# Moving 32 sample rows out of a pass of their own into the last prompt group, which is halved (groups of 4, 4, 4, 2 and 2 + sample tiles)

## The reference, cut to what matters

```python
xn = rmsnorm(x, g_mix);  z = xn @ w_in
a, u, v, ga, gb = split(z)                    # widths 512, 512, 512, 1024, 1024
pa = pool_mixer(a, hist, ...)                 # causal windows 2, 4, 8, 16; 15 rows of history
pb = u * (w_spatial (lower triangle) @ rmsnorm(v, g_v) + b_spatial)   # inside chunks of 128 rows
merged = sigmoid(ga) * (pa @ w_up_pool) + sigmoid(gb) * (pb @ w_up_gmlp)
h  = x + merged @ w_out
hn = rmsnorm(h, g_ffn)
y  = rmsnorm(h + moe(hn), g_final)            # 16 experts: best group of 4, then 2 experts in it
```

## Time and profile before

| what | value |
|---|---|
| median of 3 executions | 2057.61 us |
| profiled execution, first to last instruction (span) | 2054.1 us |
| PE busy / share | 1895.9 us / 92% |
| PEld busy / share | 1600.8 us / 78% |
| DVE busy / share | 1034.9 us / 50% |
| ACT busy / share | 832.3 us / 41% |
| mean granted TensorE clock | 0.962 |
| DMA, over the span | 153 GB/s |

### The profile page before, as it was taken

How to read it: one execution, slowest core, us unless ns; L and a number is a source line. 1 busy time by engine, 2 the same in 40 slices (tenths; PEclk the granted TensorE clock), 3 DMA queues, 4 the chain that set the end, 5 groups by cost and what they waited for, 6 DMA issues and landing times. The chain is left out here.

```text
span 2054.1 us, 28746 instructions
## 1 busy us (share of the span) xinstructions
PE 1895.9 (92%) x9892; PEld 1600.8 (78%) x9893; DVE 1034.9 (50%) x2051; ACT 832.3 (41%) x1564; POOL 283.8 (14%) x388
## 2 busy tenths in 40 slices
PE   6999999999999999999997764999999999999980
PEld 5788888888878888888885543888888888888870
DVE  4644455544454544555444654454456454546434
ACT  4333333333343333333323553444446454446423
POOL 2000000010000010000100202222222222222223
PEclk9999999999999999999997886999999999999995
DMA  6332333323342223522334575585566576656428
GB/s 213 123 100 85 139 140 132 103 92 135 123 145 96 90 83 131 173 77 95 103 123 166 169 250 168 149 268 162 155 224 218 169 264 191 184 174 215 142 53 340
DMA packets 173306, 316.24 MB, mean 154 GB/s; under 512 B 9757, under 2 KB 92701, under 8 KB 173226
## 3 DMA queue, kind: packets, MB, share of 16 engines
q1 hardware_dynamic: 155754, 255.07, 36.0%
q0 software_dynamic: 15120, 51.59, 10.1%
q10 hardware_dynamic: 2352, 8.52, 1.0%
HBM read 266.09 MB, written 49.07 MB: 153 GB/s over the span
## 5 line engine op out<-in xcount | busy, mean ns | idle before, releaser
L751 DVE TENSOR_TENSOR wl<-raw,wh 128x512 fp32r<-128x512 f32 x440 | 274.3, 685 | 207.2 <-ACT wh L573 205.3
L1597 PE MATMUL bank<-gu_hi,ex_hi 128*128 128x256 f32 (+1 forms) x960 | 310.5, 323 | 4.5 <-DVE gu_lo L1507 4.5
L60 PE MATMUL bank<-xT_hi,wh 128*128 128x512 f32 x768 | 301.0, 392 | 10.6 <-ACT ext L711 7.0
L1599 PE MATMUL bank<-gu_hi,ex_lo 128*128 128x256 f32 (+1 forms) x960 | 307.1, 320 | 0.0
L1598 PE MATMUL bank<-gu_lo,ex_hi 128*128 128x256 f32 (+1 forms) x960 | 306.9, 320 | 0.0
L62 PE MATMUL bank<-xT_hi,wl 128*128 128x512 f32 x768 | 299.4, 390 | 0.0
L61 PE MATMUL bank<-xT_lo,wh 128*128 128x512 f32 x768 | 299.3, 390 | 0.0
L573 ACT ACTIVATE wh<-raw 128x512 fp32r<-128x512 f32 x440 | 240.2, 619 | 99.5 <-PE bank L1140 49.9
L1597 PEld LDWEIGHTS bank<-gu_hi,ex_hi 128*128 128x128 f32 x960 | 183.2, 191 | 23.9 <-DVE gu_lo L1507 6.5
L1599 PEld LDWEIGHTS bank<-gu_hi,ex_lo 128*128 128x128 f32 x960 | 183.2, 191 | 13.3
L1598 PEld LDWEIGHTS bank<-gu_lo,ex_hi 128*128 128x128 f32 x960 | 183.5, 191 | 12.5
(11 more groups left out here) (239 smaller groups left out, 3258.0 us busy)
## 6 DMA issues: line engine op xcount, KB each, us to landing
raw<-in_w_in SPq DMA_DIRECT2D x70, 1024.0 KB
raw_gate_up<-in_w_gate SPq DMA_DIRECT2D x16, 2048.0 KB, 8.4
raw_gate_up<-in_w_up SPq DMA_DIRECT2D x16, 2048.0 KB, 13.4
raw_d<-in_w_down SPq DMA_DIRECT2D x16, 2048.0 KB, 13.0
raw<-in_w_out SPq DMA_DIRECT2D x20, 1024.0 KB
raw<-in_w_up_pool SPq DMA_DIRECT2D x20, 512.0 KB
raw<-in_w_up_gmlp SPq DMA_DIRECT2D x20, 512.0 KB
h<-in_x_prompt SPq DMA_DIRECT2D x16, 512.0 KB, 5.2
```

The source lines that it names most:

```text
L60: nc.tensor.matmul(out, lh, rh, start=(i == 0), stop=False)
L751: lo = lambda out, x, hi: tt(out, x, hi.bitcast(F32), ALU.subtract)
L1597: nc.tensor.matmul(out, a[0][:, ka, :], w[0][:, kw, cols], start=(n == 0), stop=False)
L1599: return nc.tensor.matmul(out, a[1][:, ka, :], w[0][:, kw, cols], start=False, stop=(n == total - 1))
```

## The change

Groups are now `PROMPT_TILES = (4, 4, 4, 2, 2)`, and the last one takes the 32 sample rows as a third, short tile: 256 + 32 = 288 columns. The number of passes (five and the prologue) and of panels stays. Group 3 has 256 columns. `sample_panel`, `to_rows` and their scratch `tm` are gone; `rows` and `rows2` depend on the tile; the prompt's and the sample's pooling rows stand side by side in `ext`, each with its 16 columns of history; the four tables of bank uses come from one function; and the loop over passes 1 and 2 is written out.

```diff
+PROMPT_TILES = (4, 4, 4, 2, 2)
+LAST = len(PROMPT_TILES) - 1
+FIRST_TILE = (0, 4, 8, 12, 14)
+def tiles_in(g):
+    return PROMPT_TILES[g] + (1 if g == LAST else 0)
...
+    @staticmethod
+    def columns(g):
+        return PROMPT_TILES[g] * P + (SAMPLE if g == LAST else 0)
...
-        def passes(eng, body):
-            body(PhaseOne(-1))
-            body(PhaseOne(0))
-            with eng.Fori(1, NPROMPT - 1) as g:
+        def passes(body):
+            for g in range(-1, LAST + 1):
                 body(PhaseOne(g))
-            body(PhaseOne(NPROMPT - 1))
-            body(PhaseOne(NPROMPT))
...
-                if not ph.pro and not ph.next:
-                    pe.wait_ge(sp_read, g * TPG + ph.nt)
-                    for i in range(2):
-                        sample_panel(ph, i, [("u", 2 * i, xT, every)])
-                    for i in range(4):
-                        sample_panel(ph, 2 + 3 * i, [("ga", 2 * i, xT, every)])
-                        sample_panel(ph, 3 + 3 * i, [("gb", 2 * i, xT, every)])
-                        pe.wait_ge(pb_ok, g * 4 + 4)
-                        sample_panel(ph, 4 + 3 * i, [("P", 2 * i, pa, [(k, k) for k in range(4)]),
-                                                     ("Q", 2 * i, pb, [(4 + k, k) for k in range(4)])])
-                elif not ph.pro:
+                if not ph.pro:
                     for i in range(2):
                         for c in range(2):
                             chunk(ph, i, c, "u", 2 * i + c, xT, every, n)
...
                 if not ph.next:
-                    router(ph, 0)
+                    router(ph, ph.nt - 1)
                     count(ph)
                     return
-                if ph.nt2 == 1:
-                    sample_panel(ph, 20, [("a", 0, xT, every)])
-                    router(ph, ph.nt - 1)
-                    sample_panel(ph, 21, [("a", 2, xT, every)])
-                    pool_products(ph, 0)
-                    pool_products(ph, 1)
-                    count(ph)
...
+                pool_products(ph, 1)
+                if ph.places_itself:
+                    count(ph)
...
                     for t in range(min(3, ph.nt)):
-                        if t == min(2, ph.nt) and ph.next:
+                        if t == min(2, ph.nt - 1) and ph.next:
                             split(ph, 19)
                         norm_h(ph, t)
...
                     b = full(act, ph, "a", m)
-                    nc.scalar.activation(exts[m % 2][:, 16:16 + n2], bankA[b][:, 0:n2], ACT.Copy)\
-                        .then_inc(a_free[b], 1)
+                    if ph.last2:
+                        nc.scalar.activation(ext[:, 32 + main:32 + main + SAMPLE], bankA[b][:, main:n2], ACT.Copy)
+                    nc.scalar.activation(ext[:, 16:16 + main], bankA[b][:, 0:main], ACT.Copy).then_inc(a_free[b], 1)
```

More of the change, by code:

```diff
@@ L63, in products, with bank_uses @@
     return last
-def bank_uses(nt, nt_next, first):
+def tiles_in(g):
+    return PROMPT_TILES[g] + (1 if g == LAST else 0)
+def bank_uses(nt, nt_next):
     seq = []
-    if not first:
+    if nt:
         seq += [("u", m) for m in range(4)]
@@ L123, in __init__ @@
-        self.before = None if self.pro else (
-            (LAST_P_USES, N_LAST_P) if static and g == NPROMPT else (MID_USES, N_MID))
+        self.pro = g < 0
+        self.next = g < LAST
+        self.nt = 0 if self.pro else tiles_in(g)
+        self.nt2 = tiles_in(g + 1) if self.next else 0
+        self.n = 0 if self.pro else self.columns(g)
+        self.n2 = self.columns(g + 1) if self.next else 0
+        self.t0 = 0 if self.pro else FIRST_TILE[g]
+        self.first = FIRST_TILE[g + 1] if self.next else NT
@@ L126, in prev, with rows, rows2 @@
+        self.last2 = g + 1 == LAST
+        self.uses, self.start = USES[g][0], USES_BEFORE[g]
+    @staticmethod
+    def columns(g):
+        return PROMPT_TILES[g] * P + (SAMPLE if g == LAST else 0)
+    def rows(self, t):
+        return SAMPLE if self.g == LAST and t == self.nt - 1 else P
+    def rows2(self, t):
+        return SAMPLE if self.last2 and t == self.nt2 - 1 else P
     @property
     def prev(self):
-        return None if isinstance(self.g, int) and (self.g < 1 or self.g == NPROMPT) else PhaseOne(self.g - 1)
+        return None if self.g < 1 or self.g == LAST else PhaseOne(self.g - 1)
@@ L131, in places_itself @@
     @property
     def places_itself(self):
-        return isinstance(self.g, int) and self.g >= NPROMPT - 1
+        return self.g >= LAST - 1
     def use(self, *key):
-        return self._place(self.uses[key])
+        i = self.start + self.uses[key]
+        return i % 2, i // 2
     def use_before(self, *key):
[L142 to L148, removed]
+        i = USES_BEFORE[self.g - 1] + USES[self.g - 1][0][key]
@@ L583, in softmaxes @@
                 act.wait_ge(exps_in, ph.g + 1)
[L584 removed]
+                nc.scalar.activation(exps[:, 0:ph.nt, :], exps[:, 0:ph.nt, :], ACT.Exp)\
                     .then_inc(exps_ok, 1)
[L587 to L595 removed]
             def squares_of_x(ph, tiles):
                 if ph.nt2 and not ph.pro:
[L599 removed]
+                    act.wait_ge(x_in, 16 * (ph.g + 1) + (16 if ph.last2 else 0))
                 for t in tiles:
```

300 lines of the change are left out of this document (123 added, 177 removed).

## The result

The changed kernel takes 2029.87 us (median of 4 runs, 2027.53 to 2030.18), the kernel before, on the same chip, 2058.71 (4 runs, 2056.06 to 2062.48). The ratio is 0.9855, 95% interval 0.984 to 0.9869. The profiled executions have spans of 2028.5 and 2054.1 us, a gain of 25.6 where 39.0 were forecast. The sign was as forecast, and the range of 2003 to 2036 held the time; it lies above the likeliest case's own range (2010 to 2028).

The account below looks back on a forecast made before the run. The sample pass was held by loading and splitting panels, the new passes by PE. Stages from 769.7 fall from 495.1 to 460.3 us, with the loop -39.0: 2015.1 profiled, median 2018.5, range 2003 to 2036 for 8 in 10.

Parts of the forecast that it names:

- The reading of the bound: Sample's u and gates: 4.5 us a panel, held by loading and splitting; in new passes PE sets the pace.
- 288 columns, 133.2 ns: Interval between 288-column matmuls, from the line through 256 and 512 columns: 0.417 ns per column plus 13 ns.
- u and gates 93 and 95.5: Passes 3 and 4: 672 matmuls each plus stalls and slow clock, 93 us (bounds 81, 104) and 95.5 (89.5, 103).
- v and hn of pass 2, 33: Two v tiles fewer, four hn tiles stay: 33 us after 31.3, nothing won; bounds 28 and 36.
- a and pooling of pass 2, 21.8: a, pooling, spatial of pass 2: fewer columns and two spatial tiles less, 34.4 us becomes 21.8.
- Pooling of pass 3, 32: Longer DVE chain +6, choose and place of two tiles -3.7, spatial +1.2: 28.5 us becomes 32; bounds 28 and 37.
- Tail, 27 and 32.4: Pass 4's tail with two more full tiles, 27 us (bounds 22, 30); then six scatters to first expert matmul, 32.4.
- Loop, -4.2: Loop over passes 1 and 2 written out: 2.65 us jump and some 1.6 of slow matmuls saved; bounds 0, -4.6.
- A: Waits smaller, clock holds: pass 2's v stretch 28, pass 3's gates 86, tail 22; 2001 us, chance 0.18.
- B: Evacuation becomes the bound: each of eight gate steps costs 3 us more, 24 in all; 2042 us, chance 0.14.
- C: 288 columns fall under the short-matmul law, 251 ns each in 780 matmuls: slower, 2110 us, chance 0.03.
- D: No gain: passes cost the same because each streams the same panels; 2058 us, chance 0.01.

Follow-up runs that it names:

- after_load_first: The changed kernel with the load of panel 20 issued ahead of all stores of h and hn; ratio 0.98 to the kernel before, span 2019.8 us.
- after_place_later: The changed kernel with group 3's rows chosen and placed between the next pass's gate steps; ratio 0.9793 to the kernel before, span 2013.6 us.
- before_unrolled: The kernel before with its loop over groups 1 and 2 written out, nothing else; ratio 0.9968 to the kernel before, span 2054.7 us.
- wide_44431: tiles_44431 with 480 matmuls of the last group's u and gates streaming 256 columns instead of 160; ratio 0.9956 to the kernel before, span 2045.8 us.
- tiles_44431: The changed kernel with groups of 4, 4, 4, 3, 1 + sample tiles, the last 160 columns; ratio 1.0203 to the kernel before, span 2101.5 us.

## Why the prediction was right, and where its sum was off

- **The reading of the bound held where the new passes are concerned.** 4.5 us a panel for 32 rows was not PE's products: a third fewer moved the stretch by 1.3 us (up to 4.7 against other executions). That it was loading and splitting alone stays open. With 48 matmuls a panel PE is the bound: a third fewer moved the two passes by 21.9. The next bound is nearer than 4.5 us a panel: with a third of the products gone the passes took 84.3 and 81.3 us, 6.0 and 5.8 a panel, with PE waiting for DVE.
- **288 columns, 133.2 ns:** 131.7 measured. u and gates 93 and 95.5: 92.8 and 94.7. In pass 4 the gaps stand in front of P1 (0.85 us in each of the four steps, behind a product on DVE), where the sum had 1.0 in front of P0. In pass 3 the sum is right and its parts are not, which is luck: 7.3 us of idle PE where 9 were counted (two gaps of 2.50 and 2.34 and five under 0.8, not three of 2.6 and one of 1.2), and 5.0 for the low clock and the rest, where 3.8 were counted.
- **v and hn of pass 2, 33:** 36.6. It lies outside the term's own bounds (28 to 36). "The v panel and then the a panel are late behind four norms" was right in kind; the term was mis-sized. What made it late was the place of the stores in SP's list, which I had not read as queued ahead of a load; moved, the stretch is 30.6.
- **a and pooling of pass 2, 21.8:** 24.3, with 2.70 us behind `ext` in front of the last a chunk. I had taken half of the matmul time off as if nothing else were in the chain; taking `ext` out of PSUM and the windows do not halve with PE's work. after_load_first and after_place_later left it standing (24.2 in the first); no run took it apart.
- **Pooling of pass 3, 32:** 35.2. DVE's choose and place were counted, the split queued behind choose (2.49 us) was not. Moving choose and place out gave 9.7. How much of the 3.2 is that split was not tested, and filling the first wait to keep the clock up gave nothing.
- **Tail, 27 and 32.4:** 28.8 and 33.8. Its transposes and routers run at clock 0.50 behind the 2.87 us for the first norm; with that wait filled the tail was 2.2 shorter. What made `dest` to the first expert matmul 1.4 longer than forecast was not tested.
- **Loop, -4.2:** the term was right. -2.4 is what the start of w_out shows, but from u of pass 1 on the loop written out gave 4.6 in before_unrolled: the gap of 2.65 and the slow matmuls behind it. The changed kernel shows 3.3 on the same way, with another stretch at the low clock in it (0.95 from 578.2 to 614.4), and came to u of pass 1 0.9 us later.
- **The rivals.** A (waits smaller, clock holds): refuted; gates of pass 3 at 92.8 and not 86, v and hn of pass 2 at clock 0.71. B (evacuation): refuted at this width, with a margin of 8.5 to 13.4 us. C (short-matmul law): refuted at 288. At 160 a matmul takes 109.2 ns at the high clock, where the line gives 79.7; of the 73.0 us by which that kernel's span is longer, wide_44431 takes back 55.7, which were the low clock, and C did not have that. D: refuted, 2029.87 and not 2058.

In short: the terms made of counted matmuls were right within 1 us. Those made of a neighbour stretch with another mix of tiles (v and hn and pooling of pass 2, pooling of pass 3, the two of the tail) were 1.4 to 3.6 us low, together 12.5 of the 14.0, all on one side. The range was built as if such misses fell to both sides by chance; that it held them is in part luck.

## What to carry to other kernels

When a pass has so few rows that PE's products do not set its time, but streaming its weights through all engines does, add its rows to a pass that PE bounds; then look at how far the second engine is behind, since halving the rows halves PE's work and none of the splits. A store that waits for a result should not stand ahead of a load in one queue. Work of a slower engine that has no hurry (choose, place) belongs beside PE's longest stretch, and no group should be so narrow that the clock stays down.

## What the hardware showed that was not expected

- **A PE without idle at the low clock.** With 160 columns the granted clock was 0.50 for 143.4 us with 143.42 busy. The Trainium skill ("TensorE: Matmul & The Clock Gate", section "HAM oscillation — how this bites in real kernels") looks for the low clock behind PE's idle gaps; this stretch has none, and the last ones before the clock fell are of 1.62 and 0.84 us. The same section advises to restructure the loop or to pad the thin dimension to 512 or more. Padding helped here and less was enough: 256 columns for 480 of the 672 matmuls gave 0.94 and 89.1 us. No run here pads to 512.
- **Narrow matmuls cost about the same: 128 and 160 columns at the high clock, 160 and 256 at the low one.** tiles_44431, 96 intervals at the low clock:

```profile
1150.21 0.41 PE L52 MATMUL bank<-xT_hi,wh 128*128 128x160 f32 x1
...
1170.69 0.41 PE L52 MATMUL bank<-pa_hi,wh 128*128 128x160 f32 x1
```

wide_44431, 12 intervals of 160 columns at the high clock (2.4 GHz):

```profile
1173.70 0.24 PE L52 MATMUL bank<-pa_hi,wh 128*128 128x160 f32 x1
...
1175.01 0.27 PE L52 MATMUL bank<-pb_hi,wh 128*128 128x160 f32 x1
```

213.3 and 109.2 ns, beside 111.5 for 128 columns in the earlier trace rows. The first 4.9 us of wide_44431's stretch have 256 columns at the low clock: 20 intervals from 1092.65 to 1096.92, 213.5 ns. So at the high clock a matmul gets 11 ns cheaper from 256 columns (119.8) down to 160 and no more, at the low clock not at all, and in a stretch of 160 alone the clock did not come back.
